# First output slab split ahead of the queries, a last norm on four columns, and output units moved between waits

## The reference, cut to what matters

```python
def hgrn2_mixer(h, w_in, lower_bound, g_norm_w, w_out):
    ...
    o = hgrn2_chunkwise(jax.nn.silu(heads(q)), 1.0 - fg, heads(i), jnp.log(fg))
    o = o * lax.rsqrt(jnp.mean(jnp.square(o), -1, keepdims=True) + RMS_EPS)
    o = o * g_norm_w.astype(jnp.float32) * jax.nn.silu(heads(g))
    return o.reshape(B, S, D).astype(h.dtype) @ w_out
```

## Time and profile before

| | |
|---|---|
| median of three runs | 2505.44 us (2505.25 to 2507.22) |
| the profiled execution | 2502.9 us, its span 2501.1 us |
| TensorE busy | 2433.5 us, 97% of the span |
| VectorE, ScalarE, GpSimd busy | 1421.4 us (57%), 925.1 us (37%), 168.1 us (7%) |
| transfers | 218.95 MB, mean 88 GB/s |
| mean granted TensorE clock | 0.995 |

### The profile page before, as it was taken

How to read it: one execution, slowest core, us unless ns; L and a number is a source line. 1 busy time by engine, 2 the same in 40 slices (tenths; PEclk the granted TensorE clock), 3 DMA queues, 4 the chain that set the end, 5 groups by cost and what they waited for, 6 DMA issues and landing times.

```text
span 2501.1 us, 31542 instructions
## 1 busy us (share of the span) xinstructions
PE 2433.5 (97%) x11766; PEld 1985.7 (79%) x11766; DVE 1421.4 (57%) x2300; ACT 925.1 (37%) x1327; POOL 168.1 (7%) x179
## 2 busy tenths in 40 slices
PE   8999999999999999999999999999999998999998
PEld 6877888888777788888778887788888877888886
DVE  6775555433776464542266765766643665766634
ACT  5443322222767332222232332533321564433312
POOL 0000000000000000000020000000030462000031
PEclk9999999999999999999999999999999999999999
DMA  4212332223112233222222112232223312323232
GB/s 145 68 60 76 97 97 96 89 93 101 59 60 68 76 101 100 93 84 93 97 89 67 50 67 84 85 101 93 92 84 103 134 52 76 101 93 101 76 116 86
DMA packets 60792, 218.95 MB, mean 88 GB/s; under 512 B 6773, under 2 KB 7061, under 8 KB 60576
## 3 DMA queue, kind: packets, MB, share of 16 engines
q1 hardware_dynamic: 58608, 208.74, 25.8%
q0 software_dynamic: 2064, 8.97, 1.0%
q10 hardware_dynamic: 32, 0.02, 0.0%
HBM read 215.59 MB, written 2.12 MB: 87 GB/s over the span
## 4 chain that ended last, share of the span: by engine, by line
PE 89%; DVE 5%; ACT 4%; issue 1%; POOL 0%; DMA 0%; DVEq 0%; SPq 0%; ACTq 0%
PE ps L254 27%; PE ps L256 27%; PE ps L255 27%; PE ps L1832 2%; PE ps L1031 2%; PE ps L1006 1%; PE ps L1017 1%; ACT window_p L1501 1%; DVE wl L248 1%; ACT wh L240 1%; DVE stick_left L1221 1%; PE ps L1856 0%; DVE window_p L1563 0%; DVE stick_p L1227 0%; PE ps L1039 0%
## 5 line engine op out<-in xcount | busy, mean ns | idle before, releaser
L254 PE MATMUL ps<-xh,wh 128*128 128x512 f32 x2000 | 796.8, 398 | 17.3 <-DVE xl L460 8.6
L256 PE MATMUL ps<-xh,wl 128*128 128x512 f32 x2000 | 781.5, 391 | 0.0
L255 PE MATMUL ps<-xl,wh 128*128 128x512 f32 x2000 | 780.2, 390 | 0.0
L240 ACT ACTIVATE wh<-raw 128x1024 fp32r<-128x1024 f32 x332 | 348.8, 1055 | 499.2 <-PE ps L256 479.4
L248 DVE TENSOR_TENSOR wl<-raw,wh 128x1024 fp32r<-128x1024 f32 x332 | 409.6, 1235 | 188.4 <-ACT wh L240 188.2
L254 PEld LDWEIGHTS ps<-xh,wh 128*128 128x128 f32 x2000 | 376.8, 188 | 98.5 <-issue 12.7
L256 PEld LDWEIGHTS ps<-xh,wl 128*128 128x128 f32 x2000 | 376.3, 188 | 80.0
L255 PEld LDWEIGHTS ps<-xl,wh 128*128 128x128 f32 x2000 | 377.1, 189 | 76.9 <-issue 2.2
L254 PE MATMUL ps<-wh,up_ah 128*128 128x512 f32 x528 | 208.6, 395 | 1.0 <-DVE wl L404 1.0
L404 DVE TENSOR_TENSOR wl<-raw,wh 128x1024 fp32r<-128x1024 f32 x56 | 80.2, 1433 | 227.6 <-ACT wh L401 227.6
L255 PE MATMUL ps<-wl,up_ah 128*128 128x512 f32 x528 | 208.3, 395 | 0.0
(11 more groups left out here) (279 smaller groups left out, 3138.8 us busy)
## 6 DMA issues: line engine op xcount, KB each, us to landing
raw<-weights SPq DMA_DIRECT2D x388, 512.0 KB, 3.5
cst<-rows_d POOLq DMA_DIRECT2D x9, 512.0 KB, 4.8
hT<-x_t SPq DMA_DIRECT2D x8, 256.0 KB, 6.3
hgrn_mask<-levels POOLq DMA_DIRECT2D x1, 2048.0 KB, 7.9
window_bias<-bias_rows POOLq DMA_DIRECT2D x1, 2048.0 KB, 9.4
out_t<-hT SPq DMA_DIRECT2D x8, 256.0 KB, 2.2
cst<-consts SPq DMA_DIRECT2D x1, 832.0 KB, 8.7
cvt<-conv SPq DMA_DIRECT2D x1, 176.0 KB, 8.6
```

The costliest lines, as they stand in the source:

```text
L240: act.activation(wh[slot][:, :], raw[slot][:, :], ACT.Copy).then_inc(hi_done, 1)
L254: pe.matmul(out, w_hi, m_hi, start=first, stop=False, **kw)
L255: pe.matmul(out, w_hi, m_lo, start=False, stop=False, **kw)
L256: return pe.matmul(out, w_lo, m_hi, start=False, stop=last, **kw)
```

## The change

Four edits. (1) In the stick and dilated stages at pair 6, both copies of slab 24 come directly behind those of slab 23. (2) At pair 7 of both stages the ten early units are done in another order: of the units for jj = 0, those of slab 26 come later, and the two of slab 24 for jj = 2 come before the second turn, with the wait for the first head's copied weights. (3) In the last hgrn pass the sum of squares is formed in four columns, root and reciprocal act on those, and four matmuls spread the result over bank 5, from which VectorE multiplies; the spread stands between early units 21 and 22. (4) Token block 3 of the window output is done ahead as well: one unit more before the second turn, and five behind the last values.

```diff
@@ heads_pe, pair 7
-            for k, t in ((1, 0), (1, 1), (2, 0), (2, 1)):
+            for k, t in ((1, 0), (1, 1)):
                 o.early_unit(pe, k, t)
+            pe.wait_ge(*a.pt_ready(2 * j + 1))
+            for t in range(2):
+                o.early_unit(pe, 0, t, 2)
             heads_turn(pe, a, j, 1)
-            pe.wait_ge(*a.pt_ready(2 * j + 1))
-            for k, t in ((0, 0), (0, 1), (1, 0)):
-                o.early_unit(pe, k, t, 2)
+            for k, t, jj in ((1, 0, 2), (1, 1, 2), (2, 0, 0)):
+                o.early_unit(pe, k, t, jj)
             heads_values(pe, a, j)
-            for k, t in ((1, 1), (2, 0), (2, 1)):
-                o.early_unit(pe, k, t, 2)
+            for k, t, jj in ((2, 1, 0), (2, 0, 2), (2, 1, 2)):
+                o.early_unit(pe, k, t, jj)
@@ stick_act; in the same way dilated_act, and stick_dve and dilated_dve with heads_lo
                 heads_hi(act, a, 3 * j + 5)
+                if j == PAIRS - 2:
+                    heads_hi(act, a, 3 * j + 6)
                 if j + 1 < PAIRS:
                     k_hi_act(act, a, j + 1)
-                    heads_hi(act, a, 3 * j + 6)
+                    if j < PAIRS - 2:
+                        heads_hi(act, a, 3 * j + 6)
                     q_hi_act(act, a, j + 1)
@@ win_out_early
-                units = [(0, 0, 2), (0, 1, 2), (1, 0, 2)] if hh == 0 else [(1, 1, 2), (2, 0, 2), (2, 1, 2)]
+                units = [(0, 0, 2), (0, 1, 2), (1, 0, 2), (1, 1, 2)] if hh == 0 else [(2, 0, 2), (2, 1, 2), (0, 0, 3)]
+                if hh == 2:
+                    units = [(0, 1, 3), (1, 0, 3), (1, 1, 3), (2, 0, 3), (2, 1, 3)]
@@ window_pe
                     win_values_pe(pe, a, j - 1)
+                if j == PAIRS:
+                    win_out_early(pe, j, 2)
@@ pe_head
-                if not proj and 26 <= c < 30:
+                if not proj and 26 <= c < 28:
+                    hgrn_out_early(pe, c - 6)
+                if not proj and c == 28:
+                    pe.wait_ge(g.rs_ready, j + 1)
+                    for b in range(SB):
+                        mm = pe.matmul(ps[:, 5, token_block(b)], g.rs[:, b:b + 1].broadcast_to([P, P]), const("ident"),
+                                       start=True, stop=True)
+                    mm.then_inc(g.rs_spread, 1)
+                if not proj and 28 <= c < 30:
                     hgrn_out_early(pe, c - 6)
...
-                if attn and c == 25:
+                if not proj and c == 25:
+                    pe.wait_ge(g.sq_ready, j + 1)
+                    for b in range(SB):
+                        mm = pe.matmul(ps[:, 5, b:b + 1], g.sq[:, token_block(b)], ones[:, 0:1], start=True, stop=True)
+                    mm.then_inc(g.sum_done, 1)
+                if attn and proj and c == 25:
@@ act_head
+                n = S if proj else SB
+                act.activation(g.root[:, 0:n], ps[:, 5, 0:n], ACT.Sqrt, scale=1.0 / P,
@@ dve_head
+                n = S if proj else SB
+                dve.reciprocal(g.rs[:, 0:n], g.root[:, 0:n]).then_inc(g.rs_ready, 1)
                 dve.wait_ge(g.og_ready, j + 1)
...
+                else:
+                    dve.wait_ge(g.rs_spread, 1)
+                    dve.tensor_tensor(g.og[:, :], g.og[:, :], ps[:, 5, :], ALU.mult).then_inc(g.gated, 1)
@@ o_win
-    ... [6, 7, 0, 1, 2, 3, 4, 5], (1, 2))
+    ... [6, 7, 0, 1, 2, 3, 4, 5], (1, 2, 3))
```

More of the change, by code:

```diff
@@ L1292, in stick_dve @@
                 heads_lo(dve, a, 3 * j + 5)
+                if j == PAIRS - 2:
+                    heads_lo(dve, a, 3 * j + 6)
                 if j + 1 < PAIRS:
@@ L1295, in stick_dve @@
                     k_lo_dve(dve, a, j + 1)
-                    heads_lo(dve, a, 3 * j + 6)
+                    if j < PAIRS - 2:
+                        heads_lo(dve, a, 3 * j + 6)
                     q_lo_dve(dve, a, j + 1)
@@ L1786, in __init__ @@
                 self.root_ready, self.rs_ready = sem("hgrn_root_ready"), sem("hgrn_rs_ready")
+                self.rs_spread = sem("hgrn_rs_spread")
                 self.og_ready, self.gated = sem("hgrn_og_ready"), sem("hgrn_gated")
@@ L1944, in act_head @@
                 act.wait_ge(g.sum_done, j + 1)
-                act.activation(g.root[:, :], ps[:, 5, :], ACT.Sqrt, scale=1.0 / P,
+                n = S if proj else SB
+                act.activation(g.root[:, 0:n], ps[:, 5, 0:n], ACT.Sqrt, scale=1.0 / P,
                                bias=small[:, 0:1]).then_inc(g.root_ready, 1)
@@ L2020, in dve_head @@
                 dve.wait_ge(g.root_ready, j + 1)
-                dve.reciprocal(g.rs[:, :], g.root[:, :]).then_inc(g.rs_ready, 1)
+                n = S if proj else SB
+                dve.reciprocal(g.rs[:, 0:n], g.root[:, 0:n]).then_inc(g.rs_ready, 1)
                 dve.wait_ge(g.og_ready, j + 1)
-                dve.wait_ge(g.rs_ready, j + 1)
-                dve.tensor_tensor(g.og[:, :], g.og[:, :], g.rs[:, :], ALU.mult).then_inc(g.gated, 1)
+                if proj:
+                    dve.wait_ge(g.rs_ready, j + 1)
+                    dve.tensor_tensor(g.og[:, :], g.og[:, :], g.rs[:, :], ALU.mult).then_inc(g.gated, 1)
+                else:
+                    dve.wait_ge(g.rs_spread, 1)
+                    dve.tensor_tensor(g.og[:, :], g.og[:, :], ps[:, 5, :], ALU.mult).then_inc(g.gated, 1)
                 dve.wait_ge(g.gated, j + 1)
@@ L2097, in program @@
         o_up2 = Tok(PH["down2"], up2.ah, up2.al, "layer", "lnfg0", "lnfb0", [7, 6, 0, 1, 2, 3, 4, 5])
-        o_win = Tok(PH["window_out"], win.oh, win.ol, "layer", "lnmg1", "lnmb1", [6, 7, 0, 1, 2, 3, 4, 5], (1, 2))
+        o_win = Tok(PH["window_out"], win.oh, win.ol, "layer", "lnmg1", "lnmb1", [6, 7, 0, 1, 2, 3, 4, 5], (1, 2, 3))
         o_up3 = Tok(PH["down3"], up3.ah, up3.al, "last", "lnfg1", "lnfb1", None)
```

## The result

| | before | after |
|---|---|---|
| median, first comparison | 2505.39 us (2505.25 to 2507.22, 4 runs) | 2493.77 us (2491.12 to 2496.28, 4 runs) |
| ratio, 95% interval | | 0.9949 [0.9934, 0.9963] |
| median, second comparison | 2506.61 us (2502.83 to 2509.67, 9 runs) | 2491.72 us (2490.81 to 2494.20, 5 runs) |
| ratio, 95% interval | | 0.9945 [0.9932, 0.9959] |
| profiled execution, span | 2502.9 us, 2501.1 us | 2494.55 us, 2492.8 us |

The change made the kernel faster by 11.6 us in the first comparison and 14.9 us in the second; the forecast was 14.1 us, to 2491.3 us. The runs scatter, from lowest to highest, by 2.0 and 6.8 us before and by 5.2 and 3.4 us after, more than it looked from the three runs shown before, and what makes it is the second half of this study.

The account below looks back on a forecast made before the run. TensorE is busy 97% of the span, so only its waits and slow matmuls could give time. Stick 3.5, dilated 5.8, hgrn 3.3 and window 1.5 sum to 14.1 us, giving 2491.3 us; range 2486.5 to 2498.5.

Parts of the forecast that it names:

- a loss at pair 6: Stick stage: the 1.24 us low-copy wait becomes one of 2.1 us for the score copies; loss 0.7 us.
- a gain at pair 7: Stick stage: reordered units fill the 3.06 us wait for slab 2 and end its slow stretch; gain 4.2 us.
- Dilated: Dilated pair 6, the largest term: earlier slab 24 copies bring the scores forward; 6.3 us at full clock, 5.8 us taken.
- half the price of slow values, 0.5 us: Dilated pair 6: deduction for a possible clock fall behind the new 2.75 us wait, lowering 6.3 to 5.8 us.
- The rival that the clock falls in the new waits: Stick, dilated and hgrn: slow clock cuts the gain from 14.1 to 9.4 us, 2496.0 us; chance 0.22.
- one of its three places: The clock rival's places and prices: stick stage 1.7 us, dilated stage 1.7 more, hgrn stretch staying slow 1.3.
- the bounds of 1.0 to 1.8: Last window pair: moved units cover the 1.52 us ready wait; gain 1.5 us, from 1.0 to 1.8.
- the one 2.18 us wait with a clock of 1.00: Dilated stage, before the next turn: full clock there was taken as evidence against clock falls in the new waits.
- the sum 11.2 us: Stick and dilated stages: if transposes don't count for the clock gate, both slow down, 3.4 us less gain; left a rival.
- 3.5 us of scatter at its low end: Range's low end, 2486.5 us: all terms at best (15.3 us) plus scatter from other waits of 1 to 2 us.
- 1.4 at its high end: Range's high end, 2498.5 us: the first two rivals plus 1.4 us of the same scatter from other waits.
- two rivals: Clock falls in new waits, 2496.0 us, chance 0.22; dilated wait only changes its name, 2497.1 us, chance 0.08.

Follow-up runs that it names:

- the split put back: Changed kernel with the stick stage's slab 24 split behind the keys again: median 2493.91 us (5 runs) against 2491.72.
- edit 2 alone: Kernel before with only the reordered early units of pair 7: 2501.21 us (10 runs), ratio 0.9991 [0.9982, 1.0001].
- the hgrn edit alone: Kernel before with only the four-column norm of the last recurrent head: 2501.59 us (12 runs) against 2505.38, ratio 0.9987 [0.9979, 0.9996].
- both fillings in the changed kernel: Changed kernel with nine unread products in each of two dilated waits, stick split put back, spread earlier: 2489.11 us (5 runs), 0.9935 against the kernel before.
- the two small edits: On the changed kernel, stick slab 24 split behind the keys again, and spread one unit earlier; run separately: 2493.91 and 2490.24 us against 2491.72.
- the kernel with the earlier spread: Changed kernel with the spread of the last recurrent norm one output unit earlier: median 2490.24 us (5 runs) against 2491.72.

## Why the prediction held, and where it was off

**What held.** Every wait that the prediction named came out. Gone: low copies at stick pair 7 and dilated pair 6. New: 1.78 us (forecast 2.1) and 2.48 us (2.75) for the copied weights, 0.50 us before the stick turn, 0.69 us (0.7) for the hgrn output. The stick stage was a loss at pair 6 (0.65 us by the split put back; forecast 0.7) and a gain at pair 7 (4.2 by edit 2 alone; forecast 4.2). Of the 4.2, 1.6 are clock: where it held behind the 3.06 us wait, as in the profile of the hgrn edit alone, turns to unit took 28.8 us (188.60 to 217.40) and not 30.45.

**The mis-sized terms.** Dilated gave 4.7 for 5.8 us. The step that failed is "half the price of slow values, 0.5 us" for the clock behind the new wait. The values cost 1.5 to 1.7 us more than at full speed in each of the six profiles that have this wait unfilled, while the new wait itself ended when forecast. That step is short by 1.2 us in the profile after (1.7 less 0.5), which is the whole of the term's error of 1.1 us. The rival that the clock falls in the new waits is therefore true in one of its three places: in the dilated stage, not behind the stick stage's 1.78 us (1.00 in the five profiles that have it) and not in hgrn (seven profiles). Its price was added up too high as well: 1.7 us "more" in the dilated stage, where 0.5 of the same 1.7 was already taken off.

The window gave 1.95 us for 1.5 (1.91 in the profile with this edit alone), outside the bounds of 1.0 to 1.8. The sum counted the 1.52 us wait alone. The unit put before the second turn also took its 0.24 us wait away: from turn to turn it was 3.28 us, and it is 3.56 us with a unit more of 0.68 us, so 0.4 us came from there. The two errors have opposite signs, so that the sum is off by 0.8 us only.

**The argument behind it was weak.** I took the one 2.18 us wait with a clock of 1.00 as a sign that waits near 2 us are harmless and 3 us are not. The trace of before already spoke against it: the clock held behind 2.52 us at 645.78, and fell at 1.68 us (1252.07) and 1.75 us (2003.20). Windows of the kernel before: length, busy PE, clock, DMA share, GB/s.

```profile
645.00:649.00 4.00, 3.22 (x31) 1.00 0.17 36
1252.00:1256.00 4.00, 3.70 (x13) 0.57 0.85 302
2003.00:2007.00 4.00, 3.80 (x10) 0.57 0.35 127
```

I read the clock behind these waits in all 14 profiles, of programs that differ only by the edits above. A stretch is counted for a wait when it began in it or up to 1.5 us after its end:

| wait | clock fell behind it |
|---|---|
| 6.88 us, dilated pair 6 | 4 of 4 |
| 3.50 us, hgrn output | 6 of 7 |
| 3.06 us, stick pair 7 | 5 of 7 |
| 2.51 us, first dilated scores | 6 of 12 |
| 2.48 us, dilated pair 6, new | 6 of 6 |
| 2.18 us, dilated pair 7 | 6 of 14 |
| 1.91 us, window values | 0 of 14 |
| 1.75 us, window queries near 2000 | 14 of 14 |
| 1.68 us, near 1250 | 14 of 14, double length in 6 |
| 1.49 us, near 1588, 1957, 2127 | 7, 0 and 3 of 14 |

One profile shows one draw of this. The length of the wait alone doesn't decide: 1.75 us always and 1.91 us never.

The price comes from the same profiles, between rows that no edit touches. From the wait near 1588 to that near 1957 it is 368.26 to 368.29 us in the seven profiles where the clock held, and 369.82 to 369.88 us in the seven where it fell: 1.6 us. From the first dilated scores to the turns of pair 6 it is 158.94 to 159.09 us in the eight without a stretch, 160.38 to 160.60 us in the six with one. A doubled stretch near 1250 costs about 2 us more than a single one.

**The rule of the Trainium skill.** The Trainium skill (TensorE: Matmul & The Clock Gate, PE-mode transpose) says that transposes don't count as busy for the clock gate. By that rule the prediction had the clock fall in both stages, and the sum 11.2 us as an estimate; it fell in one. The transposes alone in the 6.88 us wait kept the clock at 1.00, as the products did, in one profile each, so the rule is not borne out where it was tried; how the clock comes up under transposes alone was not tried. The Trainium skill (TensorE: Matmul & The Clock Gate, Part 1: The HAM clock gate) says that how many matmuls run slowly at a kernel's start varies from run to run of one kernel. The traces agree at the start (slow until 13.41 and 14.13 us), and in mid-kernel the stretches vary between the two profiles of the changed kernel.

**The sum against the median.** The terms of the profiled execution sum to 13.3 us, the medians give 11.6 and 14.9 us, and the intervals of the ratios reach from 9.3 to 16.5 and from 10.3 to 17.0 us. So the 2.5 us that the first median seemed to be short are not a finding, and how near the medians came to 14.1 us is in part luck. Shown is that an execution has stretches at the 1.2 GHz level behind some waits, that these change from one execution of a program to the next, and that each costs 1.3 to 1.7 us. The timed runs say that this is the scatter. Over 78 runs of the kernel before, taken beside the experiments, the time follows the mean granted clock of the run:

| mean granted clock | runs | time, us | median, us |
|---|---|---|---|
| 0.995 | 24 | 2501.50 to 2504.74 | 2503.3 |
| 0.994 | 24 | 2503.88 to 2506.81 | 2504.8 |
| 0.993 | 7 | 2506.28 to 2507.84 | 2507.3 |
| 0.992 | 23 | 2506.11 to 2509.68 | 2508.3 |

Not all of it is waits in mid-kernel: from the first matmul to the turns of stick pair 6, which no edit touches, the 14 profiles have 179.4 to 181.7 us. The range had 3.5 us of scatter at its low end and 1.4 at its high end. The nine runs of after went the other way, from 0.5 us under the forecast to 5.0 over it (2490.81 to 2496.28 us), and stayed inside only because the high end also had room for two rivals.

**Open.** Filling the wait of the kernel before saved 2.3 us at its place and nothing to be seen in the median, while both fillings in the changed kernel, with 1.2 us from the two small edits, took 2.6 us off, of which about 1.4 us is left for the fillings, or 0.5 us when the kernel with the earlier spread is taken as the measure. Whether a stretch saved at one place makes one at a later place likelier, and so how much a wait's filling is worth in general, isn't settled; nor is what makes the 1.75 us wait fall always and the 1.91 us wait never.

## What to carry to other kernels

When a stage waits for a copy that another engine makes last, look what stands ahead of it in that engine's list and what it would delay; here moving it forward gained 4.7 us in the stage where the next work waited anyway and lost 0.65 us in the one where it didn't. Price a wait with its clock, and take that from the chance over many profiles, not from one row. Judge an edit of a few microseconds by the distance between two rows around it; the median is right for the whole, but the runs under it differ by clock stretches at places that the edit never touched (8.2 us over the 78 runs of the kernel before).

## What the runs showed of the hardware

- A reciprocal of 128 x 512 numbers on VectorE took 3.35 us, one of 128 x 4 took 0.18 us; the spread that it then needs, four matmuls against the identity, held TensorE for 0.8 us (1543.65 to 1544.46).
- The square root on ScalarE needed a table load of 1.28 us ahead of it (1541.22) and took 0.26 us itself on four columns: the load is the larger part of what the short norm asks of ScalarE.
- 52 transposes or 26 products whose results nobody reads kept the granted clock at 1.00 over a wait of 6.9 us, the transposes with 0.98 us left idle at the end, in one profile each; with the wait unfilled it fell in four of four.
- Two executions of one program had slow stretches behind different waits of 1.5 to 2.5 us. Over 14 profiles a stretch cost 1.3 to 1.7 us, and the shorter wait could be the one it followed: 1.75 us 14 times of 14, 1.91 us never.
